# Memory cross-attention: queries behind the mix on unnormalised x, values behind them, heads between their units

## The reference, cut to what matters

```python
def rms_norm(x, g):
    y = xf * lax.rsqrt(jnp.mean(xf * xf, axis=-1, keepdims=True) + RMS_EPS)
    return (y * g.astype(jnp.float32)).astype(x.dtype)

def memory_cross_attention(h, mem_n, w_xq, w_xkv, w_xo):
    q = (h @ w_xq).reshape(bsz, seq, X_HEADS, X_HEAD_DIM)
    k, v = jnp.split(mem_n @ w_xkv, 2, axis=-1)
    ...
    s = jnp.einsum("bshd,bmhd->bhsm", q, k).astype(jnp.float32) * (X_HEAD_DIM ** -0.5)
    pr = jax.nn.softmax(s, axis=-1).astype(h.dtype)
    o = jnp.einsum("bhsm,bmhd->bshd", pr, v).reshape(bsz, seq, D_MODEL)
    return o @ w_xo

    h = h + memory_cross_attention(rms_norm(h, norm_xattn_g[l]), mem_n, w_xq[l], w_xkv[l], w_xo[l])
    h = h + conv_ffn(rms_norm(h, norm_ffn_g[l]), w_up[l], ...)
```

## Time and profile before

| | us |
|---|---|
| median of 3 runs | 2197.41 |
| lowest, highest | 2195.94, 2201.75 |
| the profiled execution | 2199.28 |
| its span, first to last instruction | 2197.5 |
| busy in it: PE | 2107.7 |
| DVE | 1653.7 |
| ACT | 1075.3 |
| POOL | 240.0 |
| mean granted clock of PE | 0.988 of full |

### The profile page before, as it was taken

How to read it: one execution, slowest core, us unless ns; L and a number is a source line. 1 busy time by engine, 2 the same in 40 slices (tenths; PEclk the granted TensorE clock), 3 DMA queues, 4 the chain that set the end, 5 groups by cost and what they waited for, 6 DMA issues and landing times.

```text
span 2197.5 us, 40176 instructions
## 1 busy us (share of the span) xinstructions
PE 2107.7 (96%) x16382; PEld 2039.2 (93%) x16382; DVE 1653.7 (75%) x2444; ACT 1075.3 (49%) x1307; POOL 240.0 (11%) x168
## 2 busy tenths in 40 slices
PE   8999999999999999999999989999999999989997
PEld 7888999999989999989999879999988999879997
DVE  7877798778769877898965658767698976648765
ACT  6766344346754434355435445444346435445442
POOL 0001045100005500002202000100001301000100
PEclk9999999999999999999999999999999999999999
DMA  6544455454235455444544424445444544424543
GB/s 249 176 159 147 142 185 189 149 201 163 105 115 176 164 192 191 159 168 154 192 155 171 173 93 176 173 157 206 174 173 152 192 173 170 157 95 173 175 157 109
DMA packets 57847, 361.61 MB, mean 165 GB/s; under 512 B 6688, under 2 KB 9312, under 8 KB 20576
## 3 DMA queue, kind: packets, MB, share of 16 engines
q1 hardware_dynamic: 57696, 359.48, 46.0%
HBM read 358.37 MB, written 1.08 MB: 164 GB/s over the span
## 4 chain that ended last, share of the span: by engine, by line
PE 87%; DVE 6%; ACT 3%; issue 3%; POOL 1%; DMA 0%; SPq 0%; DVEq 0%; ACTq 0%; POOLq 0%
PE acc L615 73%; PE acc L614 6%; ACT w_hi L1907 3%; DVE w_lo L1095 2%; PE pA L710 1%; PE pA L965 0%; PE acc L903 0%; PE pA L1038 0%; PE pB L1038 0%; POOL in_lo L2479 0%; PE pB L989 0%; PE pD L1049 0%; PE pC L1049 0%; PE pA L717 0%; PE pC L755 0%
## 5 line engine op out<-in xcount | busy, mean ns | idle before, releaser
L615 PE MATMUL acc<-in_hi,w_hi 128*128 128x256 f32 x4784 | 1348.8, 287 | 46.1 <-issue 18.6
L615 PE MATMUL acc<-in_hi,w_lo 128*128 128x256 f32 x4784 | 1335.4, 284 | 0.0
L615 PE MATMUL acc<-in_lo,w_hi 128*128 128x256 f32 x4784 | 1272.6, 284 | 2.9 <-POOL in_lo L2479 2.9
L1095 DVE TENSOR_TENSOR w_lo<-raw,w_hi 128x2048 fp32r<-128x2048 f32 (+1 forms) x349 | 757.7, 2171 | 309.9 <-ACT w_hi L1907 308.6
L1907 ACT CAST w_hi<-raw 128x2048 fp32r<-128x2048 f32 (+1 forms) x349 | 630.5, 1807 | 732.7 <-PE acc L615 677.2
L615 PEld LDWEIGHTS acc<-in_hi,w_hi 128*128 128x128 f32 x4784 | 923.9, 193 | 55.7 <-issue 27.6
L615 PEld LDWEIGHTS acc<-in_hi,w_lo 128*128 128x128 f32 x4784 | 923.1, 193 | 0.2
L615 PEld LDWEIGHTS acc<-in_lo,w_hi 128*128 128x128 f32 x4784 | 885.3, 193 | 4.7 <-POOL in_lo L2479 3.4
L2479 POOL TENSOR_TENSOR in_lo<-arena,in_hi 128x256 f32 (+2 forms) x112 | 145.2, 1296 | 1275.3 <-ACT in_hi L2351 523.4
L1720 DVE SCALAR_TENSOR_TENSOR arena<-arena,cols 128x256 f32<-128x256 f32 x480 | 200.4, 491 | 0.0
L2189 ACT CAST in_hi<-arena 128x256 f32 (+1 forms) x88 | 35.8, 407 | 185.3 <-POOL arena L2489 99.0
(11 more groups left out here) (268 smaller groups left out, 1435.1 us busy)
## 6 DMA issues: line engine op xcount, KB each, us to landing
raw<-in_wide SPq DMA_DIRECT2D x285, 1024.0 KB, 4.8
raw<-in_narrow SPq DMA_DIRECT2D x64, 704.0 KB, 4.0
arena<-cs_rows SPq DMA_DIRECT2D x16, 256.0 KB, 5.8
arena<-in_mem SPq DMA_DIRECT2D x3, 1024.0 KB, 6.9
x<-in_x SPq DMA_DIRECT2D x4, 256.0 KB, 6.6
raw<-in_wide SPq DMA_DIRECT2D x2, 512.0 KB, 6.4
tables<-in_tables SPq DMA_DIRECT2D x1, 1024.0 KB, 14.2
arena<-cs_rows SPq DMA_DIRECT2D x16, 64.0 KB, 5.9
```

The source lines that it names most:

```text
L615: return mm(outs[m], w[:, k, at], moving[:, c, :], start=start, stop=stop)
L1095: tt(w_lo[g % 2][:, 0:n], raw[g % RAW][:, 0:n], w_hi[g % 2][:, 0:n], ALU.subtract).then_inc(lo_ready, 1)
```

## The change

The weights of the queries now come ahead of those of the values. The mix's residual writes early parts (x times gain, at chunk 0), and all four query units work on them; `x_query` scales each bank by `rstd` and by the softmax's 1/16 on its way to `x_q`. The normalised x of this sublayer, with its high and low parts, is gone, and so is one "norm" entry of `pieces`. Attention goes by whole heads: four score matmuls fill a bank, one maximum for both halves (negated, so no scaling step), two exponentials, two scalings, four transposes into `pC`, one copy to a buffer of its own for each head. These steps are issued between units: scores of heads 0 and 1 behind query units 2 and 3, of heads 2 and 3 behind value units 0 and 1; the turn of head 0 behind query unit 3, of heads 1 to 3 behind value units 0 to 2; the outputs of heads 0 and 1 behind value unit 2; those of heads 2 and 3 inside the first output unit, whose matmuls are done by chunks (`some_chunks`, which the first stack's `some` now calls with what it did before). The diff, without the lines that only renumber norms or that are shown in the kernel above:

```diff
@@ -81,7 +81,7 @@
               ("ret_v", "tok_pair", DC // 2, 8, MIXER_AT), ("ret_g", "feat", DC, 8, MIXER_AT),
               ("gates", "feat", DC, 8, MIXER_AT), ("ret_out", "deep", 16, 8, RET_AT), ("mem_k", "feat", DC, 4, MEM_AT), ("conv_out", "feat", DC, 4, CONV_AT),
               ("mix", "feat", DC, 4, MIX_AT)]
-        s += [("mem_v", "tok_pair", DC // 2, 4, MEM_AT), ("mem_q", "feat", DC, 4, XN_AT), ("mem_o", "feat", DC, 4, HEADS_AT)]
+        s += [("mem_q", "feat", DC, 4, XN_AT), ("mem_v", "tok_pair", DC // 2, 4, MEM_AT), ("mem_o", "feat", DC, 4, HEADS_AT)]
         s += [("up_b", "feat", DC, FC, 0), ("down", "pair", FC // 2, 16, DC)]
     return s
@@ -291,8 +291,8 @@
         x_q = view(0, DC, T)
         x_k = view(2048, DC, T)
         x_v = view(4096, TT, D)
-        x_p = view(6144, 2, T)
-        x_pt = view(6656, TT, T)
+        x_p = view(6144, 2, TT, T)
+        x_pt = view(7168, XH, TT, T)
         mem_t = view(0, DC, T)
         cs_rows = nc.dram_tensor("cs_rows", (TT, HEADS_S * P), F32, kind="Internal").ap()
         rope_c, rope_s = tables[0:2 * ROPE, 0:T], tables[0:2 * ROPE, T:2 * T]
...
@@ -429,7 +429,7 @@
         n = NORM_PIECES
         pieces = [("norm", n), ("groups", GROUPS_S), ("norm", n), ("hid", FC)]
         pieces += [("norms", 2 * n), ("heads", ATT_H), ("norm", n), ("hid", FC)]
-        pieces += LAYERS2 * [("norm", n), ("ret", 8), ("memory", n), ("conv", 2), ("mix", 4), ("norm", n), ("xheads", XH),
+        pieces += LAYERS2 * [("norm", n), ("ret", 8), ("memory", n), ("conv", 2), ("mix", 4), ("xheads", XH),
                              ("norm", n), ("hid", FC)]
         piece, made, count = {}, {}, {"all": 0, "vector": 0, "pool": 0}
         for name, n in pieces:
@@ -443,6 +443,9 @@
             return [acc[g % 4][:, m * T:(m + 1) * T] for m in range(2)]
+        def scaled_units(nth):
+            return EARLY * (nth + 1 - (nth > 4) - (nth > 7))
         def unit_bank(seg, j):
             return acc[(seg.base + j) % (2 if seg.name == "att_q" else 4)]
...
@@ -697,6 +699,26 @@
                         last.then_inc(unit_done, 1)
                 return seg, body, groups
+            def some_chunks(seg, u, ks, back, high, low):
+                g = seg.base + u
+                if ks[0] == 0:
+                    pe.wait_ge(hi_ready, g + 1)
+                    pe.wait_ge(lo_ready, g + 1)
+                    pe.wait_ge(acc_free, g - back)
+                hi, lo = (w[g % 2][:].rearrange("p (k n) -> p k n", k=DC) for w in (w_hi, w_lo))
+                pe.wait_ge(inh_ready, high)
+                pe.wait_ge(in_ready, low)
+                for m in range(2):
+                    out, at = acc[g % 4][:, m * T:(m + 1) * T], slice(m * P, (m + 1) * P)
+                    for k in ks:
+                        c = seg.chunk0 + k
+                        mm(out, hi[:, k, at], in_hi[:, c, :], start=k == 0 and m == 0, stop=False)
+                        mm(out, hi[:, k, at], in_lo[:, c, :], start=False, stop=False)
+                        last = mm(out, lo[:, k, at], in_hi[:, c, :], start=False, stop=k == DC - 1 and m == 1)
+                if ks[-1] == DC - 1:
+                    last.then_inc(unit_done, 1)
             def project(name, second_half=None, after=None, needs=None, **early):
                 seg, body, _ = units(name, second_half, after, needs, **early)
                 if seg.kind == "pair":
...
@@ -1030,50 +1036,77 @@
                     project("mix", needs=parts("mix", l, 4, 2, gin_ready))
                 return run
...
+            def x_scores(l, h):
+                pe.wait_ge(acc_free, [s.base for s in segs if s.name == "mem_q"][l] + h + 1)
+                if h >= 2:
+                    pe.wait_ge(xexp_a, XH * l + h - 1)
+                for t in range(TT):
+                    for c in range(2):
+                        last = mm((pA, pB)[h % 2][:, t * T:(t + 1) * T], x_q[:, 2 * h + c, t * P:(t + 1) * P], x_k[:, 2 * h + c, :],
+                                  start=c == 0, stop=c == 1)
                 last.then_inc(xsc_mm, 1)
+            def x_turn(l, h):
+                pe.wait_ge(xpn_v, XH * l + h + 1)
+                if XH * l + h:
+                    pe.wait_ge(xpt_a, XH * l + h)
+                for t in range(TT):
+                    for s in range(TT):
+                        last = transpose(pC[:, s * T + t * P:s * T + (t + 1) * P], x_p[:, h % 2, t, s * P:(s + 1) * P], ident[:])
+                last.then_inc(xpt_mm, 1)
             def x_out(l, h):
...
+                pe.wait_ge(xpt_a, XH * l + h + 1)
+                pe.wait_ge(acc_free, [s.base for s in segs if s.name == "mem_v"][l] + (2 if h < 2 else 4))
+                if h == 1:
+                    pe.wait_ge(xexp_a, XH * l + XH)
                 if h >= 2:
...
+                    pe.wait_ge(in_ready, made["xheads"][l] + h - 1)
                 for c in range(2):
                     at = h * XHD + c * P
                     for s in range(TT):
...
+                        last = mm((pD, pB)[h % 2][:, c * T:(c + 1) * T], x_v[:, s, at:at + P], x_pt[:, h, s, :],
                                   start=s == 0, stop=s == TT - 1)
                 last.then_inc(xo_mm, 1)
             def cross(l):
                 def run():
...
+                    def queries(u, j):
+                        if j >= 2:
+                            x_scores(l, j - 2)
+                        if j >= 3:
+                            x_turn(l, j - 3)
+                    def values(u, j):
+                        if j < 2:
+                            x_scores(l, j + 2)
+                        if j < 3:
+                            x_turn(l, j + 1)
+                        if j == 2:
+                            x_out(l, 0)
+                            x_out(l, 1)
+                    project("mem_q", after=queries, early=4 + 3 * l, early_at=XN_AT, stats=norm_stats, wide_tail=True)
+                    project("mem_v", after=values)
+                    seg, unit, _ = units("mem_o")
+                    def some(u, ks):
+                        some_chunks(seg, u, ks, 3, piece["xheads"][l] + ks[-1] // 2 + 1, made["xheads"][l] + ks[-1] // 2 + 1)
+                    some(0, (0, 1, 2, 3))
+                    x_out(l, 2)
+                    x_out(l, 3)
+                    some(0, (4, 5))
+                    some(1, (0, 1))
+                    some(0, (6, 7))
+                    some(1, (2, 3, 4, 5, 6, 7))
+                    E.passed(in_ready, XH)
+                    for u in range(2, seg.units):
+                        unit(u, u)
                 return run
...
+            ffn_b = lambda l: ffn("up_b", 4 + 2 * l, 5 + 3 * l)
             stages(mamba, ffn("up_a", 1, 0), attention, ffn("up_a", 2, 2), second=lambda l: (mixer(l), cross(l), ffn_b(l)))
             norm_stats()
...
@@ -1116,7 +1149,7 @@
                     if nth is not None and fixed and u < EARLY:
                         if u >= 2 and not behind:
                             scale_unit(seg, nth, u)
-                        dve.wait_ge(early_v, EARLY * (nth + 1) + u + 1)
+                        dve.wait_ge(early_v, scaled_units(nth) + u + 1)
                     if first:
                         dve.wait_ge(unit_done, u + (seg.base + 1))
                         first(u, j, banks)
...
@@ -1835,46 +1868,65 @@
                         tt(y, y, gate[:, bass.ds(u * 2, 2), :], ALU.add).then_inc(val_ready, 1)
                     project("conv_out", mixed, steps={v_order: 1}, early=True)
                     E.passed(inh_ready, 4)
...
+                    residual("mix", 4 + 3 * l, f"x_norm{l}", XN_AT)
                 return run
...
+            def x_query(l, seg, u):
+                dve.wait_ge(unit_done, seg.base + u + 1)
+                stt(out=x_q[:, 2 * u:2 * u + 2, :], in0=acc[(seg.base + u) % 4][:].rearrange("p (m l) -> p m l", m=2),
+                    scalar=XHD ** -0.5, in1=rstd[:].unsqueeze(1).broadcast_to([P, 2, T]), op0=ALU.mult, op1=ALU.mult
+                    ).then_inc(acc_free, 1)
+            def x_max(l, h):
+                b = h % 2
+                dve.wait_ge(xsc_mm, XH * l + h + 1)
+                nc.vector.reduce_max(small[:, 2 * b:2 * b + 2], (pA, pB)[b][:].rearrange("p (t m) -> p t m", t=TT), AX_X, negate=True
+                                     ).then_inc(xmx_v, 1)
+            def x_scaled(l, h):
+                b = h % 2
+                dve.wait_ge(xexp_a, XH * l + h + 1)
+                E.mark(recip(small[:, 8 + 2 * b:10 + 2 * b], small[:, 4 + 2 * b:6 + 2 * b]))
                 E.settle()
...
+                E.mark(ts(x_p[:, b, 0, :], x_p[:, b, 0, :], small[:, 8 + 2 * b:9 + 2 * b], None, ALU.mult))
+                ts(x_p[:, b, 1, :], x_p[:, b, 1, :], small[:, 9 + 2 * b:10 + 2 * b], None, ALU.mult).then_inc(xpn_v, 1)
+            def x_low(l, h):
+                dve.wait_ge(inh_ready, piece["xheads"][l] + h + 1)
+                at = HEADS_AT + 2 * h
```

(68 more changed lines are left out.)

137 lines of the change are left out of this document (14 added, 123 removed).

## The result

| | before | changed |
|---|---|---|
| median, us | 2197.80 (4 runs, 2195.94 to 2201.75) | 2165.02 (4 runs, 2163.47 to 2167.04) |
| ratio, 95% interval | | 0.9849, 0.9832 to 0.9866 |
| the profiled execution | 2199.28 | 2163.47 |
| its span | 2197.5 | 2161.7 |

The changed kernel is faster by 32.8 us at the medians, 1.5%. The gain is 31.9 to 33.9 us in three comparisons, where 28.6 was forecast. The two profiled executions are further apart, 35.8 us.

The account below looks back on a forecast made before the run. PE (TensorE), busy 96% of the span, was taken to bound the kernel. Its two cross-attention stretches would fall from 199.21 to 170.58 us, gaining 28.6: 2168.8 against the median shown, called 2170, range 2165 to 2180.

Parts of the forecast that it names:

- new stretch: Memory cross-attention, first query matmul to first feed-forward matmul: 85.29 us a layer, from 98.81 and 100.40 before.
- join: First query unit straight behind the mix, on unnormalised x, with the stats matmul in it: 7.02 us.
- turn: The four transposes of one head's softmax on PE: 0.35 us, four heads 1.40 us a layer.
- the stop before unit 2: Output projection: PE idles 0.25 us until VectorE's split gives unit 2 its weights.
- returns: Slower first projection matmul behind a group of transposes: 0.09 us each, six a layer, 0.54 us.
- covers: Added VectorE and ScalarE work, costed at nothing because it should finish under PE's matmuls, slack 0.3 to near 5 us.
- the slack of 2 us: Softmax scaled 5.5 us after the unit's end, its transposes come at 7.5; head 3 has slack 2 us.
- head 2's low part: Output projection: ready about 6.1 us behind the last value unit, PE asks at 6.4; slack 0.3 us.
- (a): Output projection starts late: PE idles 2.46 us, then runs slower; 4.9 us a layer, 2178.6 us; chance 0.12.
- (b): Attention's transposes and outputs still wait for the softmax: each layer keeps its 4.7 us, 2178.2 us; chance 0.08.
- (d): A semaphore count holds scores until all queries or values are through; only the query wait goes, 2192.4 us; chance 0.04.
- (c): Small pauses from first scores to last outputs bring PE's 1.2 GHz level: 40 us a layer, 2250 us; chance 0.02.

Follow-up runs that it names:

- Experiment 4: Changed kernel with each head's transposes directly behind its own scores, not one unit later; stretch 109.0 us, kernel 2219 us (one run).
- experiment 7: Changed kernel with three other leads of the output projection: no interleaving 86.26 us a stretch, unit 1 whole 86.14, middle chunks asked for head by head 84.81.
- before_again: Second profile of the kernel before, unaltered; stretches 101.86 and 99.10 us.
- before_filled: Kernel before with unread constant transposes in PE's attention waits: 24 at the query copy, 8 at each of four turns; ratio 0.9978, median 2193.20.
- experiment 2: Kernel before, unaltered, profiled twice more; the two stretches sum to 199.2, 201.0 and 199.2 us over its three profiles.
- experiment 6: Kernel before with unread constant transposes keeping PE at work, first in the attention (ratio 0.9978), then also behind the values (stretches 98.24 and 98.26 us).
- lead_by_heads: Changed kernel with outputs of heads 2 and 3 after two chunks of output unit 0, middle chunks asked for head by head, unit 1 whole; ratio 0.9851.
- before_all_filled: before_filled with 32 more constant transposes in the 3.3 us wait between last value and first query unit; stretches 98.24 and 98.26 us, ratio 0.9977.

## Why the prediction was right or wrong

**The new stretch was right.** 85.29 forecast, 85.32 measured in both layers. By its terms: join 7.02, measured 7.00; scores of a head 1.74, measured 1.54 to 1.73; turn 0.35, measured 0.36 to 0.43; outputs 1.73 a head, measured 1.54 to 1.73; value units as before; the stop before unit 2 forecast at 0.25, measured 0.46. Scores and outputs came a little cheaper, returns a little dearer than 0.09 (up to 0.2), and this evened out. That the sum hits to 0.03 us is in part that luck.

**The covers held.** VectorE's scaling and maximum cost PE nothing. Experiment 4 tests what was said of the turns: without a unit between, each waits 3.7 us, so a unit of 5.5 and more leaves the slack of 2 us that was forecast. The tightest place was named rightly too: head 2's low part, forecast 0.3 us ahead of PE, came 0.15 ahead; experiment 7 made it late by a change of one group.

**The rivals.** (a) did not come: 0.46 us where it had 4.9 a layer. (b) did not come. (d) fell with the waits. (c), the slower side, fell as well: clock 1.00 in both stretches in all three profiles. The argument against it was thinner than it looked, though. It leaned on a lower level that came behind 2.5 us of standing still. At the end of each mixer PE waits only 1.13 and 1.47 us, in every profile, and behind that the clock fell in some: in `before_again` it was 0.52 from 1871 to 1878 us.

The Trainium skill, "TensorE: Matmul & The Clock Gate", "A second HAM failure mode: psum-queue depth-cycling", tells of a kernel whose clock swung while its groups of matmuls cycled through PSUM banks with small pauses between them. Here projections in four banks alternate with fp32 groups in four others, and the trace does not show it (1.00); but PE's pauses are 0.7 us in all, so this kernel does not test one that pauses at each group. The Trainium skill, "TensorE: Matmul & The Clock Gate", "HAM oscillation — how this bites in real kernels", tells of a kernel in which each wait of PE was followed by work at the lower level. The trace agrees in experiment 4 (four waits of 3.7 us, clock 0.91) and in `before_filled` (3.3 us of waiting, then 0.51), and not in the four stretches of experiment 2 in which the clock was 1.00 behind the same 3.3 us.

**The step that failed is what the sum left out, and with it the range.** The gain was forecast as 199.21 - 170.58 = 28.6 us, from the one stretch in each layer, and it came out as 31.9 to 33.9. The size of the gain was off, not its mechanism. Two terms were wrong:

- The old stretches stood at 98.81 and 100.40, the values of one profile. Three profiles have 199.2, 201.0 and 199.2 for the two, so the mean gain there is 199.8 - 170.6 = 29.1.
- Everything outside the stretches was put at nothing, without a reason. From the end of the first stretch to the start of the second, the same matmuls took 569.9, 572.5 and 572.5 us in the three profiles of before and 569.8 in all three of the changed kernel: 1.8 us less on average. Where it took 572.5 in `before_again`, the clock was low behind the two waits at the mixer's end. From matmul 9000 to the end of layer 0's mix it took 38.7, 36.0 and 36.0 us before and 37.3, 37.3 and 37.5 changed, 0.5 us more on average.

"Below, no join loss, no returns and no stall would save 1.3 + 0.54 + 0.25 a layer more, 4.2 us: 2165" took the range's lower end from the terms of the new stretch alone, so none of this was in it. The forecast also rounded 2168.8, the sum against the median, up to 2170, without a reason from a row; 2168.8 - 4.2 is 2164.6.

That the stretches of the profiled pair give the forecast 28.6 again says only that the new ones were right, as the old ones are the same numbers in both. And of the pair's 35.8 us, much is chance: 5.8 come from matmul 9000 (1184.05 against 1178.26), and 1.4 from layer 0's mix: 28.6 + 5.8 + 1.4 = 35.8. The first stack's time does not follow the kernel: in the fourteen profiles with the same code up to there, matmul 9000 came between 1176.9 and 1186.5 us, on average at 1181.0 in the six with the old order and at 1181.2 in the eight with the new one.

**What stays open.** The profiles place 29.1 + 1.8 - 0.5 = 30.4 us behind matmul 9000. The medians of the three comparisons give 32.8, 33.9 and 31.9, with intervals that begin at 29.5, 30.6 and 28.8. An estimate from every execution whose granted clock is listed points at the clock for the rest: span times (1 - clock) is 24.9 us on average over 50 executions of before and 16.1 over 14 of the changed kernel. These 8.8 us less, with the 24.6 of waits and cheaper turns from experiment 6, make 33.4. Experiment 6 finds 4.6 of the 8.8 in the stretches, and 1.8 lie between them, less 0.5 in layer 0's mix. Where the other 2.9 lie is open, and so is how a change in these stretches moves the slow ones elsewhere: `lead_by_heads`, with a clock of 1.00 in both stretches, has 572.4 us between them, and `before_all_filled` has 569.8.

## What to carry to other kernels

Where PE stands still for a softmax, put whole units of another projection between its steps, one unit between the scores and their use: the waits go, and so does the slow clock behind them, which in the worst case here cost more than half as much again as the waits themselves (8.9 beside 14.8 us). Price a new order by the distance from start to start of the same groups elsewhere in the trace; it held to 0.03 us in 85. But take the old order's time from more than one profile before drawing a range, and that of the stages around it too, as the parts that wait are the parts that vary.

## What the runs showed of the hardware that was not expected

Work on PE that nobody needs made the kernel faster. The 88 transposes a layer took the clock of the old stretches from 0.95 to 0.98 up to 1.00, and the ratio of `before_all_filled` is 0.9977 (0.9967 to 0.9986), about 5 us, though eight of them delay PE by 0.63 us.

The same wait does not always bring the lower clock. Behind 3.3 us of waiting ahead of the queries it was 1.00 in four stretches of the unaltered kernel before, 0.76 and 0.50 in two.

A switch of ScalarE's function table cost only its own load. The timeline of ScalarE in the changed kernel, at the first exponential of layer 0 (start, duration):

```profile
1236.27 1.28 ACT L2476 ACT_TABLE_LOAD   x1
1237.57 0.47 ACT L2476 ACTIVATE arena<-pA,small 128x256 f32<-128x256 f32 x1
```

The exponential starts 1.30 us behind the start of the load. The Trainium skill, "ScalarE: Activation LUTs", "What ACT_TABLE_LOAD costs", gives the load 1283 ns and adds about 1380 ns of draining for each switch. The load agrees, 1.28 us; of a drain behind it the trace shows nothing, and ahead of it the conversion of the weights (1234.36, 1.90 us long) had ended at 1236.26, 0.01 us before the load. It is the same all over this profile: of the 53 loads behind another instruction of ScalarE, 49 have the next one within 0.02 us of their end. PE did not wait for this exponential, as no turn in these stretches of the changed kernel has a wait.
